# A recurrence on TensorE: where the projection steps stand between the small products

## The reference

```python
def rwkv7_scan(r, decay, k, v, kk, a):
    def step(S, inp):
        r_t, w_t, k_t, v_t, kk_t, a_t = inp
        sa = jnp.einsum('bhij,bhj->bhi', S, -kk_t)
        S = (S * w_t[:, :, None, :]
             + sa[..., None] * (kk_t * a_t)[:, :, None, :]
             + v_t[..., None] * k_t[:, :, None, :])
        y = jnp.einsum('bhij,bhj->bhi', S, r_t)
        return S, y
...
def rwkv_attention_mixer(h, w_in, mu, ...):
    proj = h @ w_in
    p_rwkv, q, k, v = jnp.split(proj, [RWKV_COLS, RWKV_COLS + ATT_WIDTH, RWKV_COLS + 2 * ATT_WIDTH], axis=-1)
    y_rwkv = rwkv7_group(p_rwkv, mu, ...)
    y_att = chunk_band_attention(q, k, v, rel_bias)
    return jnp.concatenate([y_rwkv, y_att], axis=-1) @ w_out
```

## Time and profile before

| | |
|---|---|
| three runs | 2378.8, 2378.81, 2381.31 us |
| profiled execution, first to last instruction | 2380.6 us |
| PE busy | 98% |
| DVE, ACT, POOL busy | 49%, 38%, 49% |
| pair 0, 1206 to 1257 us | PE busy 48.92 of 51 us, granted clock 1.00 |
| pair 1, 1257 to 1317 us | PE busy 56.15 of 60 us, granted clock 0.94 |
| pair 2, 1317 to 1369 us | PE busy 40.08 of 52 us, granted clock 0.86 |
| pair 3, 1369 to 1423 us | PE busy 50.06 of 54 us, granted clock 0.89 |

### The profile page before, as it was taken

How to read it: one execution, slowest core, us unless ns; L and a number is a source line. 1 busy time by engine, 2 the same in 40 slices (tenths; PEclk the granted TensorE clock), 3 DMA queues, 4 the chain that set the end, 5 groups by cost and what they waited for, 6 DMA issues and landing times.

```text
span 2380.6 us, 36961 instructions
## 1 busy us (share of the span) xinstructions
PE 2327.4 (98%) x13968; PEld 1906.4 (80%) x13968; DVE 1162.0 (49%) x1781; ACT 909.5 (38%) x1444; POOL 1165.6 (49%) x685
## 2 busy tenths in 40 slices
PE   8999999999999999999999799999999999999998
PEld 7888887888888888878876677888888887888887
DVE  4432146268634321376554546613625986731732
ACT  5332125467743321265553314212233435321222
POOL 5444445554565454445364415444445983544442
PEclk9999999999999999999999889999999989999999
DMA  4222222310032222232110003222222232222231
GB/s 163 97 97 97 90 96 106 124 54 1 15 102 98 96 97 97 89 122 81 62 47 29 29 2 106 94 92 96 97 88 91 89 106 80 97 97 88 97 96 54
DMA packets 56125, 200.08 MB, mean 84 GB/s; under 512 B 6224, under 2 KB 6480, under 8 KB 56016
## 3 DMA queue, kind: packets, MB, share of 16 engines
q1 hardware_dynamic: 54432, 195.82, 24.2%
q10 hardware_dynamic: 1584, 2.75, 0.4%
HBM read 196.45 MB, written 2.10 MB: 83 GB/s over the span
## 4 chain that ended last, share of the span: by engine, by line
PE 51%; DVE 2%; ACT 1%; issue 0%; POOL 0%; DVEq 0%; POOLq 0%; ACTq 0%
PE ps L129 15%; PE ps L131 15%; PE ps L130 14%; PE ps L1992 1%; PE ps L636 1%; PE ps L1968 0%; PE ps L1988 0%; PE ps L651 0%; PE ps L2668 0%; PE ps L1931 0%; PE ps L2039 0%; PE ps L1857 0%; DVE sb_aq L998 0%; PE ps L1953 0%; DVE sb_ak_lo L1002 0%
## 5 line engine op out<-in xcount | busy, mean ns | idle before, releaser
L110 POOL TENSOR_TENSOR sb_w_lo<-sb_w_raw,sb_w_hi 128x1024 fp32r<-128x1024 f32 (+1 forms) x361 | 890.5, 2469 | 944.7 <-ACT sb_w_hi L97 943.5
L129 PE MATMUL ps<-sb_xn_hi,sb_w_hi 128*128 128x512 f32 x1688 | 667.0, 395 | 2.7 <-DVE sb_xn_lo L171 2.7
L130 PE MATMUL ps<-sb_xn_lo,sb_w_hi 128*128 128x512 f32 x1688 | 658.9, 390 | 0.0
L131 PE MATMUL ps<-sb_xn_hi,sb_w_lo 128*128 128x512 f32 x1688 | 658.3, 390 | 0.0
L97 ACT ACTIVATE sb_w_hi<-sb_w_raw 128x1024 fp32r<-128x1024 f32 x362 | 380.1, 1056 | 491.1 <-PE ps L131 465.1
L129 PEld LDWEIGHTS ps<-sb_xn_hi,sb_w_hi 128*128 128x128 f32 x1688 | 316.9, 188 | 73.6 <-issue 3.6
L131 PEld LDWEIGHTS ps<-sb_xn_hi,sb_w_lo 128*128 128x128 f32 x1688 | 317.0, 188 | 67.7
L130 PEld LDWEIGHTS ps<-sb_xn_lo,sb_w_hi 128*128 128x128 f32 x1688 | 317.1, 188 | 66.4 <-issue 1.7
L131 PE MATMUL ps<-sb_hid_hi,sb_w_lo 128*128 128x512 f32 x864 | 344.2, 398 | 0.0
L129 PE MATMUL ps<-sb_hid_hi,sb_w_hi 128*128 128x512 f32 x864 | 339.4, 393 | 1.8 <-DVE sb_hid_lo L397 1.8
L130 PE MATMUL ps<-sb_hid_lo,sb_w_hi 128*128 128x512 f32 x864 | 340.6, 394 | 0.0
(11 more groups left out here) (444 smaller groups left out, 3008.9 us busy)
## 6 DMA issues: line engine op xcount, KB each, us to landing
sb_w_raw<-weights SPq DMA_DIRECT2D x365, 512.0 KB, 3.5
sb_stage<-x SPq DMA_DIRECT2D x4, 512.0 KB, 4.9
sb_abias<-table ACTq DMA_DIRECT2D x8, 256.0 KB, 4.1
out<-sb_out_stage SPq DMA_DIRECT2D x8, 256.0 KB, 2.9
sb_lora_w<-lora ACTq DMA_DIRECT2D x2, 256.0 KB, 2.7
sb_par<-params SPq DMA_DIRECT2D x1, 231.0 KB, 6.5
sb_ctaps<-dw ACTq DMA_DIRECT2D x1, 124.0 KB, 2.0
```

What stands on the lines that cost most here:

```text
L110: pool.tensor_tensor(c.w_lo[:, slot, 0:width], c.w_raw[:, slot, 0:width], c.w_hi[:, slot, 0:width].bitcast(F32), ALU.subtract).then_inc(c. ...
L129: pe.matmul(out, hi, rhs_hi(k0 + k), start=first, stop=False)
L130: pe.matmul(out, hi, rhs_lo(k0 + k), start=False, stop=False)
L131: mm = pe.matmul(out, lo, rhs_hi(k0 + k), start=False, stop=last)
```

## The change

In each pair the steps 3 to 16 are drawn into fewer places. The number of steps, their order and all other instructions stay.

| place | steps before | steps after |
|---|---|---|
| after `prod`, after `lab` | 0 and 1; 2 | the same |
| after `lv` (level 0) | 3 | 3, 4 |
| level 1 | 4 | none |
| level 2 | 5 | 5, 6 |
| level 3 | 6 | none |
| level 4 | 7 | 7 |
| ahead of the last E | 8 | none |
| after `z` | 9 | 8, 9, 10 |
| after `g` | 10 | none |
| after `s2` to `s7` | 11, 12, 13, 14, 15, 16 | 11 and 12 after `s3`, 13 and 14 after `s5`, 15 and 16 after `s7` |
| after `y` | from 17 | the same |

```diff
@@ -1973,13 +1973,15 @@
                     mm = pe.matmul(ps[across(s, p), 4 + s, block(b)], w.M[HALF[p], s, b, 2], w.tok[HALF[p], 3, b, HALF[s]],
                                    start=True, stop=True)
                 done("lv", mm)
-                fill(j, 3, 4)
+                fill(j, 3, 5)
                 tail(t, "var")
                 prepare(q, "lora_a")
             elif lv == 2:
                 prepare(q, "kkb")
-            if lv >= 1:
-                fill(j, 3 + lv, 4 + lv)
+            if lv == 2:
+                fill(j, 5, 7)
+            elif lv == 4:
+                fill(j, 7, 8)
             V(j, f"W{lv}")
             if lv == 0:
                 A(j, "lv")
@@ -1993,7 +1995,6 @@
                                start=True, stop=True)
             done(f"e{lv}", mm)
 
-        fill(j, 8, 9)
         V(j, f"E{len(LEVELS) - 1}")
         for b, s, p in tiles():
             mm = pe.matmul(ps[HALF[p], 4 + s, block(b)], w.E[across(s, p), s, b], w.tok[across(s, p), 0, b, HALF[s]],
@@ -2003,7 +2004,7 @@
             mm = pe.matmul(ps[HALF[p], 6 + s, block(b)], w.E[across(s, p), s, b], w.LV[across(s, p), b, HALF[s]], start=True,
                            stop=True)
         done("z", mm)
-        fill(j, 9, 10)
+        fill(j, 8, 11)
         tail(t, "yrb")
 
         A(j, "u")
@@ -2015,7 +2016,6 @@
             mm = pe.matmul(ps[HALF[s], 6 + p, block(b)], w.U[HALF[p], b, HALF[s]], w.tok[HALF[p], 1, b, HALF[s]],
                            start=True, stop=True)
         done("g", mm)
-        fill(j, 10, 11)
         V(j, "ru")
         for b, s, p in tiles():
             pe.matmul(ps[HALF[s], 4 + p, block(b)], w.Z[HALF[p], b, HALF[s]], w.M[HALF[p], s, b, 1], start=True, stop=False)
@@ -2039,7 +2039,8 @@
                 mm = pe.matmul(ps[HALF[s], 6, ch % 2 * HD:ch % 2 * HD + HD], w.G[HALF[s], ch - 1], w.S[HALF[s], ch - 1],
                                start=True, stop=True)
             done(f"s{ch}", mm)
-            fill(j, ch + 9, ch + 10)
+            if ch % 2 == 1:
+                fill(j, ch + 8, ch + 10)
         V(j, f"S{NCH - 1}")
         for ch in range(1, NCH):
             for s in range(2):
```

## The result

Six runs of each kernel: 2388.32 us after (2387.45 to 2389.71) against 2380.30 before (2378.8 to 2381.8). The ratio is 1.0033, with a 95% interval of 1.0021 to 1.0044: **slower by 8.0 us**. The forecast was 2386.1 us, 7.3 above its base, within 2380.5 to 2390.5. The traced execution after is the slowest of its six (2389.71 us). That of before has no time on record; where a run has both, its span is 1.7 to 2.1 us under its time, so by its span of 2380.6 us it took some 2382.5 us, more than any of its six. The two traces compare as their kernels do, 7.2 us apart.

The account below looks back on a forecast made before the run. PE, busy 98% of the span, was taken as the bound, so only its waits or clock matter. Pairs 0, 1, 3 add 2.63 + 1.49 + 3.14 = +7.3 us to 2378.8: 2386.1 us, range 2380.5 to 2390.5.

Parts of the forecast that it names:

- Lone steps in the levels are free: Levels: a lone step fills PE's wait for DVE's W; `w` to `d` 1.52 us with, 1.51 without; removal costs 0.
- A second step costs 0.69: Levels 0 and 2: a second step adds 0.69 us; pair 0's level 2 taken as +0.45, its scan absorbing some.
- Two steps more after `z`: Behind `z`, two steps more: +1.38 us in pairs 0 and 3, +0.99 in pair 1, where `yrb` waits 0.39.
- `yl` comes earlier: After `g`, without its step, `yl` starts earlier: -0.46 us in pair 0, -0.2 in pairs 1 and 3.
- States, three times 0.19: Chain of states: two groups take 2.49 us instead of 2.30, three times +0.19, +0.57 in pairs 0, 1 and 3.
- Pair 1: Step 4 free in the wait ahead of `var`; -0.56 level 1, +0.69 level 2, +0.99, -0.2, +0.57: +1.49 us.
- that rival: Pair 1's shorter idle, 1.98 us, keeps the clock up: sum 4.6, 2383.4 us; chance 0.13.
- Pair 2, nothing: Pair 2 draws no steps, so the change costs it 0.
- Pair 3: Level 0 +1.3 at low clock, level 1 -0.6, level 2 +0.69, +1.38, -0.2, +0.57: +3.14 us.
- more falls of the clock: New 0.8 us waits per level make the clock fall more, each about 3.3 us: 2389.4 to 2392.7 us; chance 0.12.
- Switching: Switching between small products and steps costs 0.3 us; 21 fewer give -6.3 us, 2372.5 us; chance 0.05.
- Hidden further on: Later waits for ACT and POOL in pairs 1 and 3 (2.67, 2.73 us) absorb the delay: 2379 us; chance 0.08.

Follow-up runs that it names:

- states: Kernel before with the change's grouping only in the chain of states (steps 11 to 16 behind s3, s5, s7): 2382.52 us, ratio 1.0007.
- levels: Kernel before with the change's grouping only from level 0 to g, the states keeping one step behind each group: 2387.47 us, ratio 1.0026.
- idle: Kernel before with pair 1's level 0 drawing steps 3 to 6, and levels 2, 3 and s2 none: 2379.88 us, ratio 0.9992.
- switch: Kernel after with step 8 moved from behind z to between u and z: one run, 2387.09 us.
- warm_grouped: Kernel before with the change's grouping everywhere, plus unread products in pair 2's wait (12) and pair 3's (9): 2384.07 us.
- warm: Kernel before plus unread 512-column products, 12 ahead of var in pair 2 and 9 ahead of step 3 in pair 3: 2376.92 us, ratio 0.9979.
- warm_idle: Kernel before with `warm`'s unread products in pairs 2 and 3 and `idle`'s step placement in pair 1: 2374.11 us, ratio 0.9972.
- warm_full: `warm_idle` plus unread products in pair 2's levels 1 to 4 and ahead of E (3 each) and behind z (6): 2373.09 us, ratio 0.9965.

## Why the prediction was right

The mechanism held, and the range; the sum was 0.7 us short of the difference, and 1.5 us more came from its base, which was the median of three runs (2378.8) where six give 2380.3. Against the traces it worked from, the sum was 2.3 us short (the pairs grew by 9.5), and that in the trace after the code ahead of the pairs and behind them ran 2.3 us shorter is luck. Its remark that the trace was 1.8 us above the median compares a span with a time; the execution was more like 3.7 us above it, as said at the result. Point by point:

- *Lone steps in the levels are free:* right. Taken away, `w` to `d` stays 1.50 us in levels 1 and 3.
- *A second step costs 0.69:* right in level 0 (+0.69). In level 2 of pair 0 it was +0.68 (from `w` to the next `w`, 4.35 against 3.67), not the 0.45 that I took. The scan did not absorb any; it took 2.35 us instead of 1.66, beside POOL.
- *Two steps more after `z`:* `u` to `ru` +1.37 in pair 0 (forecast 1.38), +0.79 in pair 1 (0.99), +1.40 in pair 3 (1.38).
- *`yl` comes earlier:* it did, 1.51 us behind `ru`, but it brought nothing in pair 0. `ru` to the product of `prepare(q, "bonus")` (L1868) is +0.11 us, where -0.46 was forecast, because PE stood 1.13 us in `h` with nothing to wait for ("issue", at 1242.78) and 0.55 before. That the sum of pair 0 still came to +2.4 is luck: `s2` starts 1.08 us behind that product and not 2.06, since DVE's copy of the first state took 0.20 us and not 1.18.
- *States, three times 0.19:* +0.58, +0.56 and +0.60 in the pairs 0, 1 and 3. Right.
- *Pair 1:* step 4 falls wholly into the wait ahead of `var`, which shrinks from 2.67 to 1.99 us. Right, and the clock fell all the same, so that rival is out. That the pair came to +1.5 for 1.49 is luck in part. From `w` of level 0 to `w` of level 1 it is 0.54 us more, where 0 was forecast, because `var` now runs at the low clock for a part (1.49 us against 0.99). `u` to `ru` (+0.79 for 0.99) and `ru` to `s2` (-0.48 for -0.2) took it back. Before, PE stood 0.79 us in `h` without a reason that shows, and not after.
- *Pair 2, nothing:* wrong by 0.9 us. `h` has an issue gap of 1.11 us, and none before; `y` to the next `prod` is 0.73 longer at the low clock; `u` to `yl` is 0.87 shorter at the higher one. No step of the change is there. Six kernels have the same instructions in this pair (before, after, `states`, `levels`, `idle`, `switch`), and it takes 50.8 to 51.8 us in their traces, so I count it to the spread between executions.
- *Pair 3:* the step at the low clock cost 1.28, forecast 1.3. The term that was mis-sized is where the clock comes back. From `d` of level 1 to `w` of level 2 it is 2.41 us against 1.79, and `w` to `d` in level 2 2.79 against 1.52, 1.27 more where 0.69 was taken: 0.62 + 0.58 = 1.2 us more than forecast. `ru` to `s2`, +0.04 instead of -0.2, is another 0.24. `levels` shows that this stretch isn't fixed by the instructions, since the same ones had the clock back more than 9 us sooner.

The rivals: *more falls of the clock* did not come as a sum. The low clock has 34.1 us before and after; it moved, some 3.8 us from pair 2 to pair 3, and pairs 0 and 3 of `warm_grouped` show the cost at the full clock. None of the signs that I had named against me came: `w` to `d` in levels 1 and 3 kept its 1.5 us and its idle 0.81, and the granted clock does not differ in sum. *Switching* is real and hidden. *Hidden further on* is out: only level 0 of pair 1 was taken up by a wait, as forecast.

What stays open: why equal code ahead of the recurrence differs by up to 2.5 us between executions, what sets the length of a stretch at the low clock, and what makes the issue gaps.

## What to carry to other kernels

Before moving filler work, look at what the engine would do without it: the same distance in a stretch without filler tells what each piece costs (here 0 us in a level, 0.50 in the chain, 0.69 behind another piece). Spread filler over the waits, one piece each, and put the longer runs only where a wait is long enough for them. And where a wait has nothing to fill it, products that nobody reads can pay, because more of what follows then runs at the full clock: 4.4 us here for 21 products in two waits, and 7.3 with three steps of pair 1 moved into its wait as well.

## What the runs showed of the hardware that I had not expected

**Some instructions of DVE and POOL exclude one another from start to end.** POOL's durations are rough, yet the cases below agree. The scan of pair 0 on DVE's timeline after, and POOL's product beside it:

```profile
1225.65 2.35 DVE L2318 TENSOR_TENSOR_SCAN sb_L<-sb_dist_local,sb_ss 128x512 f32<-128x512 bf16 x1
```

```profile
1225.62 1.29 POOL L2238 TENSOR_TENSOR sb_y<-sb_y,sb_rkk 128x512 f32<-128x512 f32 x1
```

And POOL's timeline of the kernel before, where the scan stood from 1226.77 to 1228.43:

```profile
1226.06 1.29 POOL L2234 TENSOR_TENSOR sb_rkk<-sb_rkk,sb_y 128x512 f32<-128x512 f32 x1
1227.43 2.08 POOL L2237 TENSOR_TENSOR sb_y<-sb_y,sb_rkk 128x512 f32<-128x512 f32 x1
```

The scan ends 1228.00 - 1226.91 = 1.09 us behind the end of POOL's product after, and 1228.43 - 1227.35 = 1.08 us before. It starts its real work when POOL is done, and its 1.66 and 2.35 us are the same 1.1 us with a wait of 0.6 and 1.3 inside. POOL's next product, of 1.29 us by itself, took 2.08 beside the scan. The Trainium skill (SBUF — State Buffer, "Who interferes with whom") says so: a DVE instruction in a two-port mode (copy, tensor_scalar), or one with two SBUF inputs against a POOL instruction that reads SBUF, shares a port pair with POOL that whoever comes first holds for the whole instruction. The rows of `warm` agree: the operation on 8 columns, 0.16 us in the kernel after, takes 1.28 where a product of POOL started 0.01 us ahead of it. DVE's copy of the first state, 1.18 us before and 0.20 after, is a third case: before, a product of POOL ran from 1243.21 to 1244.48, and the copy ended at 1244.54. Not every pair of instructions does so: beside POOL's product of 1.27 us at 1341.40 in the kernel after, DVE's L2416, which reads PSUM and one tile of SBUF, took its usual 0.68 us (at 1341.36). On a chain such as D's, this is a cost that moves with every shift of the timing.

**Issue gaps.** In `yl` and `h`, 64 small products in a row (128 rows of the trace), PE stands at most once, for up to 1.5 us, with nothing to wait for that the profile shows, at a place and of a length that change: 0.55 us in pair 0 before, 1.13 after, 0.98 in `levels`; in pair 1 0.79 before, none after, 1.51 in `states`. Between two executions this is as much as a term of the sum.

**The clock.** Idle of 3.57, 2.73, 2.67 and 1.99 us was followed by a fall to the lower level, and so was one of 0.61 us in `idle`; one of 0.64 us in `warm` was not, though products of 512 columns ran right ahead of both. Nor do those products settle it: with the same ones and the same 0.64 us in `warm_idle` and 0.63 in `warm_grouped`, the clock fell 2.0 and 2.9 us behind the start of `var`. The fall comes inside the wait or up to 3 us behind it. The return came some 3 us (`levels`) and 12.4 us (the kernel after) behind the start of pair 3's step 3, with the same instructions. The products nobody reads made the low stretches fewer and shorter (13.7 us in `warm`, 10.2 in `warm_idle` and `warm_full`, of 34.1 before), but did not rule a fall out.
